# Mixture-of-experts stage: a nine-unit loop, with the two-half units in the third place of two rounds in three

## The reference, cut to what matters

```python
def expert_block(args):
    xb, e = args                       # a block of up to 128 tokens of expert e
    return (jax.nn.silu(xb @ w1[e]) * (xb @ w3[e])) @ w2[e]
yb = lax.map(expert_block, (buf.reshape(n_blocks, EXPERT_BLOCK, d), block_expert))
y_rows = yb.reshape(-1, d)[dest] * wts.reshape(-1)[order][:, None].astype(t.dtype)
return jnp.zeros_like(t).at[tok].add(y_rows)
```

## Time and profile before

| | us |
|---|---|
| median of 3 runs | 1176.0 (1174.67 to 1176.15) |
| profiled execution, its time | 1176.18 |
| profiled execution, its span | 1174.2 |
| loop of the experts, TensorE | 751 to 1147 |
| sums, norm and output | 1147 to 1174 |

### The profile page before, as it was taken

One profiled execution on the slowest core, in us unless ns is written; L12 is line 12 of the kernel. 1 busy time (PEld: TensorE's weight loads), 2 busy tenths in 40 slices (PEclk: granted clock), 3 DMA queues, 4 the chain that ended last, 5 costly groups with the idle time before them and its releaser, 6 DMA issues.

```text
span 1174.2 us, 16137 instructions
## 1 busy us (share of the span) xinstructions
PE 1101.4 (94%) x5701; PEld 702.1 (60%) x5701; DVE 562.2 (48%) x1010; ACT 317.1 (27%) x539; POOL 167.6 (14%) x237
## 2 busy tenths in 40 slices
PE   6999999989999999999999998899999999987785
PEld 4798878868667777777888776333333333322223
DVE  5776677744676788676554447211111112111114
ACT  4642322244334544333433243000000000000004
POOL 0000000000110323345000100121212122211110
PEclk9999999999999999999999998899999999999999
DMA  9433545620111222232133559989999999999975
GB/s 384 185 114 121 215 163 214 244 98 19 54 55 54 73 73 77 86 113 104 54 107 108 214 203 392 426 319 421 421 426 425 417 425 416 425 427 426 426 324 226
DMA packets 41334, 278.16 MB, mean 237 GB/s; under 512 B 7482, under 2 KB 7994, under 8 KB 29376
## 3 DMA queue, kind: packets, MB, share of 16 engines
q1 hardware_dynamic: 34496, 264.95, 56.4%
q0 software_dynamic: 6784, 12.49, 2.9%
HBM read 274.11 MB, written 13.40 MB: 245 GB/s over the span
## 4 chain that ended last, share of the span: by engine, by line
PE 75%; DMA 12%; DVE 7%; ACT 3%; issue 2%; SPq 0%; DVEq 0%; POOL 0%; ACTq 0%; POOLq 0%
PE psum L702 72%; DMA ering<-in_wb 6%; DMA ering<-in_wa 2%; DMA ada<-in_adaw 2%; PE psum L718 1%; DVE amx L1793 1%; DMA xr<-token_rows,tabt 1%; DVE sc L1782 1%; DVE ring_lo L1522 1%; PE psum L1044 1%; ACT ring_hi L1225 1%; PE psum L740 1%; DMA gat<-expert_rows 1%; DMA Hx<-in_xT 1%; DVE sg L1522 0%
## 5 line engine op out<-in xcount | busy, mean ns | idle before, releaser
L702 PE MATMUL psum<-ering,xs 128*64 128x512 f32 x1056 | 239.5, 604 | 24.6 <-DMA ering<-in_wa 12.3
L702 PE MATMUL psum<-Hhi,ring_hi 128*128 128x512 f32 x472 | 189.5, 402 | 0.1
L702 PE MATMUL psum<-Hlo,ring_hi 128*128 128x512 f32 x472 | 185.4, 393 | 0.2 <-DVE Hlo L1522 0.2
L702 PE MATMUL psum<-Hhi,ring_lo 128*128 128x512 f32 x472 | 183.2, 390 | 0.0
L702 PEld LDWEIGHTS psum<-ering,xs 128*64 128x64 f32 x1056 | 73.2, 138 | 168.1 <-issue 134.1
L1522 DVE TENSOR_TENSOR ring_lo<-ring,ring_hi 128x1024 fp32r<-128x1024 f32 x87 | 107.1, 1231 | 114.3 <-ACT ring_hi L1225 113.2
L1522 DVE TENSOR_TENSOR sg<-sg,psum 128x256 f32<-128x256 f32 x66 | 27.8, 421 | 258.6 <-ACT sg L1225 257.5
L702 PE MATMUL psum<-ering,at 128*64 128x512 f32 x528 | 119.4, 597 | 0.7 <-DVE ysb L1522 0.7
L1225 ACT ACTIVATE ring_hi<-ring 128x1024 fp32r<-128x1024 f32 x87 | 92.2, 1060 | 75.1 <-DMA ring<-in_stream 46.9
L702 PEld LDWEIGHTS psum<-Hhi,ring_hi 128*128 128x128 f32 x472 | 88.7, 188 | 23.4 <-issue 4.0
L702 PEld LDWEIGHTS psum<-Hhi,ring_lo 128*128 128x128 f32 x472 | 88.5, 188 | 19.8
(11 more groups left out here) (353 smaller groups left out, 1449.5 us busy)
## 6 DMA issues: line engine op xcount, KB each, us to landing
ering<-in_w SPq DMA_DIRECT2D x28, 2048.0 KB, 16.1
ering<-in_wb SPq DMA_DIRECT2D x28, 2048.0 KB, 19.9
ering<-in_wa SPq DMA_DIRECT2D x28, 2048.0 KB, 15.9
ring<-in_stream SPq DMA_DIRECT2D x87, 512.0 KB, 4.2
ada_ring<-in_stream SPq DMA_DIRECT2D x32, 512.0 KB, 3.7
ada<-in_adaw SPq DMA_DIRECT2D x4, 2048.0 KB, 10.4
Am<-decay_rows POOLq DMA_DIRECT2D x8, 512.0 KB, 4.2
gat<-expert_rows SPq DMA_DIRECT2D x4, 1024.0 KB, 9.1
```

What stands on the lines that cost most here:

```text
L702: return nc.tensor.matmul(out, lhsT, rhs, start=start, stop=stop)
```

## The change

The body of each loop is three rounds (TRIO = 9 steps) long in place of one. Heavy units take the third place of the second and the third round of each trio, so the first heavy unit is unit 5, then 8, 14, 17 and 23 for five of them. MAXU becomes (MAXH + 1) // 2 * TRIO = 72, and NTAB, the columns of the table, goes from 102 to 162. In heavy steps the second half's `act_turn` and ScalarE's `act_columns` for it come after the next unit's `up_and_gate`. In a trio step whose number of heavy places k is nh or more (here units 25, 26 and 27), `down` and `rows_out` come first in the step, ahead of the next unit's `up_and_gate`. Some small tiles move to other addresses, the column numbers come from `umap` in place of `rows`, and n is at least 4.5 nh + 1.5. SyncE's loop keeps its form, but ROUNDS is 24.

```diff
 SLOTS = 3
 MAXH = 2 * S // (BLK // 2 + 1)
-MAXU = SLOTS * MAXH
+TRIO = 3 * SLOTS
+MAXU = (MAXH + 1) // 2 * TRIO
...
-NTAB = 2 * (MAXU + 6)
-UM = 3 * NTAB
+NTAB = 2 * (MAXU + TRIO)
+UM = 4 * NTAB
...
-        with pe.Fori(0, ROUNDS) as i:
-            for q in range(SLOTS):
-                u, j = i * SLOTS + q + 1, (q + 1) % SLOTS
-                here, then = i * 16 + 16 * (1 + (q == 2)), i * 16 + 16 * (1 + (q > 0))
+        with pe.Fori(0, MAXU // TRIO) as i:
+            for q in range(TRIO):
+                u, j = i * TRIO + q + 1, (q + 1) % SLOTS
+                here, then = i * 48 + 16 * ((q + 1) // SLOTS + 1), i * 48 + 16 * ((q + 2) // SLOTS + 1)
+                heavy, k = q in (4, 7), i * 2 + (q > 5)
                 with pe.If(u < n):
                     act_turn(0, u + 1)
-                    if j == SLOTS - 1:
-                        with pe.If(i < nh):
-                            up_and_gate(1, j, i + 1, here)
-                            tokens_in(1, i + 2)
-                            act_turn(1, i + 1)
+                    if heavy:
+                        with pe.If(k < nh):
+                            up_and_gate(1, j, k + 1, here)
+                            tokens_in(1, k + 2)
+                    with pe.If(k >= nh):
+                        down(0, j, u + 1, here)
                     with pe.If(u + 1 < n):
                         up_and_gate(0, (j + 1) % SLOTS, u + 2, then, True)
-                        tokens_in(0, u + 1)
-                    if j == SLOTS - 1:
-                        with pe.If(i < nh):
-                            down(1, j, i + 1, here)
-                    down(0, j, u + 1, here)
+                        if not heavy:
+                            tokens_in(0, u + 1)
+                    if heavy:
+                        with pe.If(k < nh):
+                            act_turn(1, k + 1)
+                        with pe.If(u + 1 < n):
+                            tokens_in(0, u + 1)
+                    with pe.If(k < nh):
+                        if heavy:
+                            down(1, j, k + 1, here)
+                        down(0, j, u + 1, here)
...
-        with act.Fori(0, ROUNDS) as i:
-            for q in range(SLOTS):
-                u = i * SLOTS + q + 1
+        with act.Fori(0, MAXU // TRIO) as i:
+            for q in range(TRIO):
+                u = i * TRIO + q + 1
+                heavy, k = q in (4, 7), i * 2 + (q > 5)
                 with act.If(u < n):
                     act_columns(0, u + 1)
-                    if q == 1:
-                        with act.If(i < nh):
-                            sigma(1, i + 1)
-                            act_columns(1, i + 1)
+                    if heavy:
+                        with act.If(k < nh):
+                            sigma(1, k + 1)
                 with act.If(u + 1 < n):
                     sigma(0, u + 2)
+                if heavy:
+                    with act.If(k < nh):
+                        act_columns(1, k + 1)
...
+                heavy, k = q in (4, 7), i * 2 + (q > 5)
+                if heavy:
+                    with v.If(k < nh):
+                        silu_times(1, k + 1)
+                        token_columns(1, k + 2)
                 with v.If(u < n):
+                    with v.If(k >= nh):
+                        rows_out(0, u + 1, u + 1)
                     with v.If(u + 1 < n):
                         silu_times(0, u + 2)
                         token_columns(0, u + 1)
-                    if q == 1:
-                        with v.If(i < nh):
-                            rows_out(1, i + 1, i + 1)
-                    rows_out(0, u + 1, u + 1)
+                    with v.If(k < nh):
+                        if heavy:
+                            rows_out(1, k + 1, k + 1)
+                        rows_out(0, u + 1, u + 1)
...
-    heavy_at = unit % SLOTS == SLOTS - 1
-    shift = _np.where(heavy_at, -1000 - unit, -((unit + 1) // SLOTS))
-    back = _np.where(heavy_at, unit - unit // SLOTS, 0)
+    heavy_at = (unit % SLOTS == SLOTS - 1) & (unit % TRIO >= SLOTS)
+    heavy_before = _np.cumsum(heavy_at) - heavy_at
+    shift = _np.where(heavy_at, -1000 - unit, -heavy_before)
+    back = _np.where(heavy_at, unit - heavy_before, 0)
```

More of the change, by code:

```diff
@@ L390, in build @@
     PT = [at("PT0", 73728 + 7680, [P, 640]), at("PT1", o, [P, 640])]; gf_at.append(o); o += 2560
+    step = at("step", 193728 + C_LE * 4, [P, 2 * NE])
+    bex = at("bex", o, [P, 2 * NE]); o += 256
     assert o <= 229368 - BASE, o
@@ L432, in build @@
     bpi = at("bpi", m0, [P, 2, 8], I32); m0 += 64
-    tabd = at("tabd", m0, [P, NTAB], U32); m0 += up(NTAB * 4)
-    tabt = at("tabt", m0, [P, NTAB], U32); m0 += up(NTAB * 4)
+    tabd = at("tabd", 193728 + C_PERM * 4, [P, NTAB], U32)
+    tabt = at("tabt", 193728 + C_PERM * 4 + up(NTAB * 4), [P, NTAB], U32)
     idx = at("idx", m0, [P, 4], U32); m0 += 32
@@ L443, in build @@
     sg = [at(f"sg{h}", m0 + 10240 * h, [P, S // 2]) for h in range(2)]
-    at_ = [at(f"at_{h}", m0 + 1024 + 10240 * h, [P, S // 2]) for h in range(2)]; m0 += 12288
+    at_ = [at(f"at_{h}", m0 + 1024 + 10240 * h, [P, S // 2]) for h in range(2)]
+    m0 += max(12288, 4096 + up(8 * NTAB * 4) + 8 * BLK * 4)
     assert m0 <= 177344, m0
@@ L2073, in _ @@
         rows_out(0, 1, 1)
-        with v.Fori(0, ROUNDS) as i:
-            for q in range(SLOTS):
-                u = i * SLOTS + q + 1
-                if q == 1:
-                    with v.If(i < nh):
-                        silu_times(1, i + 1)
-                        token_columns(1, i + 2)
+        with v.Fori(0, MAXU // TRIO) as i:
+            for q in range(TRIO):
+                u = i * TRIO + q + 1
+                heavy, k = q in (4, 7), i * 2 + (q > 5)
[3 more added lines that the diff above has]
+                        token_columns(1, k + 2)
                 with v.If(u < n):
+                    with v.If(k >= nh):
+                        rows_out(0, u + 1, u + 1)
                     with v.If(u + 1 < n):
@@ L2215, in _ @@
         for h in range(2):
-            gather_at(h, tabt[:, 2 * EARLY + h:2 * EARLY + h + 1])
+            first = (2 * EARLY, 4 * SLOTS - 1)[h]
+            gather_at(h, tabt[:, first:first + 1])
         for h in range(2):
             g_.wait_ge(xt_full[h], 1)
-            gather(h, (slice(2 * SLOTS, 2 * SLOTS + 1), slice(4 * SLOTS - 1, 4 * SLOTS))[h], 2)
+            gather(h, (slice(2 * SLOTS, 2 * SLOTS + 1), slice(2 * TRIO - 1, 2 * TRIO))[h], 2)
         g_.wait_ge(route_done, 3)
@@ L2223, in _ @@
         rows_home_at(0, slice(0, 1), 2)
-        with g_.Fori(0, ROUNDS) as i:
-            for q in range(SLOTS):
-                u = i * SLOTS + q + 1
+        with g_.Fori(0, MAXU // TRIO) as i:
+            for q in range(TRIO):
+                u = i * TRIO + q + 1
+                heavy, k = q in (4, 7), i * 2 + (q > 5)
                 with g_.If(u < n):
[L2228 to L2231, removed]
+                    if heavy:
+                        with g_.If(k < nh):
+                            g_.wait_ge(xt_full[1], k + 2)
+                            gather(1, bass.ds(u * 2 + 2 * TRIO + 1, 1), k + 3)
                     with g_.If(u + 1 < n):
@@ L2234, in _ @@
                         gather(0, bass.ds(u * 2 + 6, 1), u + 2)
-                    if q == 1:
-                        with g_.If(i < nh):
-                            rows_home_at(1, bass.ds(i * (2 * SLOTS) + 2 * SLOTS - 1, 1), i + 2)
+                    if heavy:
+                        with g_.If(k < nh):
+                            rows_home_at(1, bass.ds(u * 2 + 1, 1), k + 2)
                     rows_home_at(0, bass.ds(u * 2, 1), u + 2)
@@ L2331 @@
     unit = _np.arange(P)
[L2332 to L2334 removed]
+    heavy_at = (unit % SLOTS == SLOTS - 1) & (unit % TRIO >= SLOTS)
+    heavy_before = _np.cumsum(heavy_at) - heavy_at
+    shift = _np.where(heavy_at, -1000 - unit, -heavy_before)
+    back = _np.where(heavy_at, unit - heavy_before, 0)
     col_u = _np.arange(NTAB) // 2
     umap = _np.concatenate([
[L2337 to L2338 removed]
+        _np.where(heavy_at, -1000, 2 * shift + 2 * unit)[col_u] + _np.arange(NTAB) % 2, (heavy_before + 1)[col_u], 2 * back[col_u],
+        _np.arange(NTAB)])
+    umap = _np.concatenate([_np.broadcast_to(umap, (P, UM)), _np.stack([shift + unit, heavy_before + 1, back, 0.5 + 0 * unit, 1.5 + 0 * unit], axis=1)],
                            axis=1).astype(_np.float32)
```

22 lines of the change are left out of this document (8 added, 14 removed).

## The result

The changed kernel takes 1179.1 us (median of 22 runs, 1176.2 to 1184.0), the kernel before 1175.9 in 22 runs measured beside it (1173.0 to 1179.4): a ratio of 1.0028, with a 95% interval of 1.0019 to 1.0038, or 3.3 us slower. The profiled execution takes 1179.78 with a span of 1177.7, against 1176.18 and 1174.2. The forecast was 1178.5: a gain of 7.4 in front of the last `down`, and a loss of about 10 behind it. Both are there.

A forecast was written before the change was run, and what follows sets the result against it. The loop is bound by the DMA weight stream, with one 5.8 us hole. Last down 7.4 earlier, but the longer walk gives 1176.18 + 2.6 - 0.57 + 0.5 = 1178.7 profiled, 1178.5 median; own range 1174 to 1183.

The forecast's parts named there:

- Part 1, light first round: First loop round: earlier slot release closes the weight stream's hole; gain 5.8 us, bounds 0 and 11.
- Part 2, turned later: Heavy steps: saves TensorE 6.8 us in all, but TensorE is not the loop's bound then; gain zero.
- Part 3, late unit 23: Near the loop's end: last heavy unit 23 leaves TensorE short of slack; cost 1.0 us, between 0 and 3.
- Part 4, down first: Last units: down of unit 26 leaves the path; last down at 1136.3, 7.4 us earlier with the parts before.
- Part 5, the table: Before the loop: 60 more table columns lengthen 16 matmuls from 2.03 to perhaps 2.3; cost 0.3 us, bounds 0 and 1.5.
- Part 6, TensorE's walk: Behind the last down: 45 skipped steps and five trips take 18.4 us; transposes of H at 1155.0, before 1152.98.
- Part 6, VectorE: Behind the last unit: five skipped trips of 3.1 us, 15.5 in all, from 1140.0; dgw at 1155.6, as before.
- Part 6, the clock: Behind the loop: TensorE idles 15 us, so its granted clock stays low longer; cost 0.5 us, between 0 and 2.
- the walk is cheap or hidden: Rival, behind the last unit: skipped steps cost nothing, the whole 7.4 us gain stays, 1168.6; chance 12%.
- The loop body no longer stays in memory: Rival, TensorE's jumps back: larger body needs instruction fetches; 1188 with one a trip, 1248 with seven; chance 23%.
- The hole moves: Rival, weight stream: the hole shifts, say to the first heavy round, and the stream ends as before; 1184, chance 12%.
- Heavy rounds were losing too: Rival, heavy rounds: late releases cost time there as well, so everything comes 5 us earlier; 1173.5, chance 8%.

The follow-up runs named there:

- before_place: Kernel before with heavy units one round later (5, 8, 11, 14, 17), three-step loop kept, nothing turned later, no down first: 1169.45 us, 0.9942.
- before_turn: Kernel before with only the second halves' act_turn and act_columns moved behind the next up product: 1174.82 us, 0.9987.
- before_down: Kernel before with only down and rows_out put first in steps of rounds without a heavy unit: 1175.47 us, 0.9995.
- before_long: Kernel before with nine more rounds (27 steps, none executed) in the loops of TensorE, ScalarE and VectorE: 1188.74 us, 1.0105.
- after_guard: Changed kernel with one more branch around each nine-step trip on TensorE, ScalarE, VectorE and GpSimd: 1169.62 us, 0.9943 against the kernel before.
- before_nine: Kernel before with its round unrolled three times in the loop body, five trips of nine steps, heavy units unmoved: 1175.57 us, 1.0001.
- place_all_guard: Kernel before, three-step loop, with heavy units from unit 5 in every round, later turn, down first and a branch around each round: 1168.66 us, 0.9934.
- before_guard: Kernel before with one more branch around each round of three steps on all four engines: 1178.22 us, 1.0017.

## Why the prediction was right, step by step

The sum of the first five terms was -7.4 and the profile has -7.2; the walk was to bring +2.6 on `Xr` and did bring 2.93; the total was to be +2.5 in the profile and is +3.6 in time (1179.78 - 1176.18). Against the runs' medians, +3.3. The mechanism, its place and its sign held. Three sizes were off, and the largest of them, VectorE's, did no harm by luck.

- **Part 1, light first round, 5.8.** Right in mechanism, about 1 too small in size: the share is 1.01 in the stretch, the last `wb` lands at 1128.3 (forecast 1129.25), 6.4 sooner than before, and 6.9 sooner in before_place, which gains 6.8 in all. The upper bound of 11 is not reached.
- **Part 2, turned later, zero.** Argued for this kernel from the share of 1.01, and not tested in it; before_turn shows 1.5 where the hole is still open.
- **Part 3, late unit 23, 1.0.** Right in TensorE's path, off in what it is compared with. `wb` of unit 23 lands at 1067.27 (forecast 1067.0), and from there TensorE never waits for weights again: it comes to the end of unit 27's up product at 1134.06 (forecast 1133.9), with 2.05 us of waits for VectorE and ScalarE in between. The last `wb` landed 0.95 sooner than forecast, so the DMA alone would have allowed 1132.0: the late unit costs 2.1 and not 1.0. The start of the last `down` (1136.51 against 1136.3) is right because it hangs on TensorE's path and not on that landing. TensorE in order of time, kernel after:

```profile
1067.27 3.65 PE L704 MATMUL psum<-ering,xs 128*64 128x512 f32 x16 [1.68 <-DMA ering<-in_wb]
...
1110.71 3.65 PE L704 MATMUL psum<-ering,at 128*64 128x512 f32 x16 [0.70 <-DVE ysb L1535]
...
1127.09 7.04 PE L704 MATMUL psum<-ering,xs 128*64 128x512 f32 x32
1134.06 0.66 PE L720 MATMUL psum<-CT,xr 128*128 128x128 f32 x4
```

- **Part 4, down first.** The last turn and copy came in 2.45 us from the up product's end to `down` as worked out (2.4), and before_down has the local 2.9. The bound on the scatter held less well: `ysb` waited 0.5 for it.
- **Part 5, the table, 0.3.** The 16 matmuls take 2.48 (forecast 2.3). No experiment took the part by itself, and TensorE comes to them at 734.2 to 735.5 in different profiles, with either table, so 0.3 can't be seen.
- **Part 6, TensorE's walk.** 19.39 from the last `down` to the transposes, forecast 18.7; the first skipped branch starts 1.2 behind the start of `down`, where before it was 0.6, which is most of the difference. ScalarE's own queue was through at 1156.5 (forecast 1156.7), and `Xr` came at 1157.05, for here TensorE's transposes were the later of the two, by half a microsecond; the prediction had ScalarE the later.
- **Part 6, VectorE, "`dgw` at 1155.6, as before".** Wrong by 2.4. A trip takes 3.35, not 3.1, so the walk with its ends is 17.3 and not 15.6, and it starts at 1140.64 and not 1140.0. It cost next to nothing, for TensorE was at the spare product until 1161.17, and `dgw` was done at 1159.27: that is luck. By these times VectorE alone would have kept most of the loss if the other two had been quick, but no run tried it.
- **Part 6, the clock, 0.5.** Mis-sized: 1.0 to 1.1. The granted clock is 0.52 over the 17.3 us behind the loop, and on the spare product (1.91) and the first rows' product (1.20) TensorE still runs at it, where before only the transposes did. From `Xr`'s start to the end it is 20.65 us against 20.1 that still held the wait of 0.57, which gives the 1.1; that all of it is the clock is inferred.

Of the rivals, *the walk is cheap or hidden* is refuted by before_long (+12.4) and by after_guard (-9.5). That the branch costs ScalarE 45 ns was no help, for 0.37 us go by a step of ScalarE all the same, most of it in no row. *The loop body no longer stays in memory* is refuted by the six packets of the first trip and by before_nine. Of what the Trainium skill's page Runtime: NRT & Kernel Launch says under Instruction fetch mechanics, the trace is in keeping with the size of 128 KiB for TensorE and not with the rule of the 2-page window: no packet of q8 comes at any of the seven jumps back. *The hole moves* is refuted by 1.01 in both stretches. *Heavy rounds were losing too* is refuted but for about 1 us. In the kernel before, TensorE's heavy rounds take 46.95 us and `wb` lands every 47.1 (823.5, 870.8, 917.9, 964.8); in place_all_guard TensorE's take 46.11, yet `wb` still lands only every 46.9 (816.2 to 956.8), and each load waits longer in the queue than the one a round ahead. So there the stream is the bound, and a faster TensorE had 0.2 a round to win.

Beyond the prediction: the first guarded kernel of before was expected to gain, as if its walk of 5.6 were a cost that could be had. It was cover. A walk costs what it adds to the 13.5 us that go by from the last `down` to the first product of the returned rows in any case: nothing before, 24.66 - 13.50 = 11.2 after.

## What to carry to other kernels

A loop of fixed length whose steps are skipped by a condition costs its skipped steps, about 0.4 us each here, on every engine and behind the last real unit, where nothing hides them once they outlast the transfer that the end waits for; when a change lengthens the trip or the bound, count the skipped steps of every engine, and put one condition around the trip. Price a gain at the end of a loop against the next wait behind it: 14.7 us of walk removed were worth 9.5, and in the kernel before the same condition cost 2 us (1.0017). And where TensorE is to wait anyway, spare products through the wait can be worth 1 to 3 us in what follows.

## What was not expected of the hardware

- A taken branch lasts 208 ns on TensorE and 45 on ScalarE, but a skipped step costs both about 0.37 us (one branch on TensorE, two on ScalarE): the branch's own duration does not price it.
- Work finished early can slow the end. After 5.7 us without products the granted clock was 0.50 over the next 3.6, and the first two products took 2.05 us in place of 1.02 to 1.10 (1.2 in place of 2.4 GHz); before_guard lost some 2 us by it (1.0017 against 1.0000 with the wait filled).
- A loop body of some 1,640 TensorE instructions (the prediction's estimate) came with six packets of q8 by the end of the first trip and none in seven more trips.
